# A weight-stationary expert form in two widths (136 and 152 rows) in a hybrid decoder trunk's MoE layer

## What is computed

```
logits = h @ w_router                      # 512 x 8
top_logit, top_e = top_k(logits, 2); gates = softmax(top_logit)
# rows are sorted by expert and padded to blocks of 128
y_block = (silu(x @ w1[e]) * (x @ w3[e])) @ w2[e]     # w1, w3: 1024 x 3584, w2: 3584 x 1024
y = sum over a row's two experts of gate * y_block row
```

## Time and profile before

| | before |
|---|---|
| median of 3 runs | 2075.96 us (2074.44 to 2076.59) |
| the profiled execution | 2074.16 us, of which the span from first to last instruction is 2072.5 us |
| PE busy | 1995.7 us (96%) |
| PE weight loads busy | 1770.0 us (85%) |
| DVE busy | 1576.3 us (76%) |
| ACT busy | 1104.1 us (53%) |
| mean DMA rate | 218 GB/s |

### The profile page before, as it was taken

How to read it: one execution, slowest core, us unless ns; L and a number is a source line. 1 busy time by engine, 2 the same in 40 slices (tenths; PEclk the granted TensorE clock), 3 DMA queues, 4 the chain that set the end, 5 groups by cost and what they waited for, 6 DMA issues and landing times.

```text
span 2072.5 us, 34371 instructions
## 1 busy us (share of the span) xinstructions
PE 1995.7 (96%) x12246; PEld 1770.0 (85%) x12247; DVE 1576.3 (76%) x1964; ACT 1104.1 (53%) x1269; POOL 89.5 (4%) x104
## 2 busy tenths in 40 slices
PE   7999999999999999999999999999999999999993
PEld 6889787877778788999999988888999888999882
DVE  6866535344468677888888899998888998888996
ACT  6532423323345423555555577777555776555773
POOL 0000000000000002100100010101000101000101
PEclk9999999999999999999999999999999999999997
DMA  5312723132312215777777699999777999776983
GB/s 195 105 59 92 265 80 119 64 121 63 119 61 92 71 52 170 250 261 259 250 252 260 231 378 368 364 379 340 270 243 244 340 378 325 254 259 235 375 318 144
DMA packets 218811, 450.97 MB, mean 218 GB/s; under 512 B 13088, under 2 KB 64304, under 8 KB 218768
## 3 DMA queue, kind: packets, MB, share of 16 engines
q1 hardware_dynamic: 210416, 421.05, 58.2%
q0 software_dynamic: 8352, 29.33, 3.8%
HBM read 432.50 MB, written 17.84 MB: 217 GB/s over the span
## 4 chain that ended last, share of the span: by engine, by line
PE 83%; DVE 10%; issue 3%; ACT 2%; DMA 1%; DVEq 0%; POOL 0%; ACTq 0%; SPq 0%; POOLq 0%
PE ps L583 17%; PE ps L585 17%; PE ps L584 17%; PE ps L925 12%; PE ps L942 8%; PE ps L927 5%; PE ps L944 3%; DVE w_lo L1777 2%; DVE w_lo L1774 1%; PE ps L652 1%; ACT w_hi L1189 1%; DVE w_lo L1331 1%; PE ps L607 1%; PE ps L846 1%; DVE ex L1356 0%
## 5 line engine op out<-in xcount | busy, mean ns | idle before, releaser
L1774 DVE TENSOR_TENSOR w_lo<-raw,w_hi 128x1024 fp32r<-128x1024 f32 x340 | 414.5, 1219 | 81.9 <-ACT w_hi L1189 79.5
L925 PE MATMUL ps<-xt,w_hi 128*128 128x320 f32 x1792 | 465.3, 347 | 2.2 <-DVE xt L1788 1.9
L927 PE MATMUL ps<-xt,w_lo 128*128 128x160 f32 x1792 | 424.2, 237 | 0.0
L1189 ACT ACTIVATE w_hi<-raw 128x1024 fp32r<-128x1024 f32 x340 | 357.4, 1051 | 112.6 <-PE ps L927 61.2
L1777 DVE TENSOR_TENSOR w_lo<-raw,w_hi 128x1024 fp32r<-128x1024 f32 x340 | 414.1, 1218 | 0.0
L1191 ACT ACTIVATE w_hi<-raw 128x1024 fp32r<-128x1024 f32 x340 | 356.4, 1048 | 0.0
L927 PEld LDWEIGHTS ps<-xt,w_lo 128*128 128x128 f32 x1792 | 343.1, 191 | 0.1
L925 PEld LDWEIGHTS ps<-xt,w_hi 128*128 128x128 f32 x1792 | 337.2, 188 | 2.8 <-issue 2.7
L583 PE MATMUL ps<-act_hi,w_hi 128*128 128x512 f32 x608 | 242.1, 398 | 5.2 <-DVE act_lo L1375 5.2
L585 PE MATMUL ps<-act_hi,w_lo 128*128 128x512 f32 x608 | 239.9, 395 | 0.0
L584 PE MATMUL ps<-act_lo,w_hi 128*128 128x512 f32 x608 | 239.9, 395 | 0.0
(11 more groups left out here) (330 smaller groups left out, 3174.7 us busy)
## 6 DMA issues: line engine op xcount, KB each, us to landing
raw<-in_moe_w_dram SPq DMA_DIRECT2D x672, 512.0 KB, 5.4
raw<-in_w_in_dram SPq DMA_DIRECT2D x19, 1024.0 KB, 5.1
raw<-in_ffn_w_gate_dram SPq DMA_DIRECT2D x11, 1024.0 KB, 5.3
raw<-in_ffn_w_up_dram SPq DMA_DIRECT2D x11, 1024.0 KB, 5.4
raw<-in_ffn_w_down_dram SPq DMA_DIRECT2D x11, 1024.0 KB, 4.9
raw<-in_w_out_dram SPq DMA_DIRECT2D x8, 1024.0 KB, 5.0
y_rows<-mult POOLq DMA_DIRECT2D x1, 8192.0 KB, 29.5
y_rows<-yacc POOLq DMA_DIRECT2D x8, 512.0 KB, 5.5
```

What stands on the lines that cost most here:

```text
L925: pe.matmul(pairs_of(ps[:, bank, 0:2 * NW]), hi_[:, k % 4, f * P:(f + 1) * P], xt[:, k, :, 0:NW], start=k == 0, stop=False)
L927: last = pe.matmul(ps[:, bank, NW:2 * NW], lo_[:, k % 4, f * P:(f + 1) * P], xt[:, k, 0, 0:NW], start=False, stop=k == KT - 1)
L1189: act.activation(slot_hi[p % 6][:, 0:half], raw6(p)[:, 0:half], ACT.Copy).then_inc(w_hi_half, 1)
L1774: dve.tensor_tensor(slot_lo[p % 6][:, 0:half], raw6(p)[:, 0:half], f32(slot_hi[p % 6][:, 0:half]), ALU.subtract)
```

## The change

The width of the turned form falls from 160 to 152 rows for everything that is allocated, copied, added or multiplied, and its limit on the second block from 32 to 24 rows. On PE alone there are two bodies of the turned item: one streams 152 rows, the other 136. The router's list says which: two more DVE operations in the chain make the flag 2 where the second block has at most 8 rows (`NARROW - P`), and 1 otherwise. The banks keep their layout in steps of `NW`; the narrow body streams the first 136 columns of each of the two halves, so its input and its output of L925 and L942 are two stretches with a gap of 16 columns. In the 152 body the two halves stay adjacent. The columns past 136 that the other engines read in a narrow item hold what was there before, and belong to no row.

```
-NW = P + 32
+NW = P + 24
+NARROW = P + 8
...
-            def turned_up(kind, f, p, c_at):
+            def turned_up(kind, f, p, c_at, nw):
...
-                    pe.matmul(pairs_of(ps[:, bank, 0:2 * NW]), hi_[:, k % 4, f * P:(f + 1) * P],
-                              xt[:, k, :, 0:NW], start=k == 0, stop=False)
-                    last = pe.matmul(ps[:, bank, NW:2 * NW], lo_[:, k % 4, f * P:(f + 1) * P],
-                                     xt[:, k, 0, 0:NW], start=False, stop=k == KT - 1)
+                    pe.matmul(pairs_of(ps[:, bank, 0:2 * NW])[:, :, 0:nw], hi_[:, k % 4, f * P:(f + 1) * P],
+                              xt[:, k, :, 0:nw], start=k == 0, stop=False)
+                    last = pe.matmul(ps[:, bank, NW:NW + nw], lo_[:, k % 4, f * P:(f + 1) * P],
+                                     xt[:, k, 0, 0:nw], start=False, stop=k == KT - 1)
...
-                    pe.matmul(pairs_of(ps[:, bank, 0:2 * NW]), hi_[:, f % 2, d * P:(d + 1) * P],
-                              ht_n[:, f, :, :], start=f == 0, stop=False)
-                    last = pe.matmul(ps[:, bank, NW:2 * NW], lo_[:, f % 2, d * P:(d + 1) * P],
-                                     ht_n[:, f, 0, :], start=False, stop=f == 3)
+                    pe.matmul(pairs_of(ps[:, bank, 0:2 * NW])[:, :, 0:nw], hi_[:, f % 2, d * P:(d + 1) * P],
+                              ht_n[:, f, :, 0:nw], start=f == 0, stop=False)
+                    last = pe.matmul(ps[:, bank, NW:NW + nw], lo_[:, f % 2, d * P:(d + 1) * P],
+                                     ht_n[:, f, 0, 0:nw], start=False, stop=f == 3)
...
             with pe.Fori(0, n_items) as n:
-                with pe.If(pe.snap(turned_next, min_val=0, max_val=1) > 0):
-                    item_turned(n)
+                form = pe.snap(turned_next, min_val=0, max_val=2)
+                with pe.If(form > 0):
+                    with pe.If(form > 1):
+                        item_turned(n, NARROW)
+                    with pe.Else():
+                        item_turned(n, NW)
                 with pe.Else():
                     item_one(n)
...
             link(dve.tensor_tensor(w3v[3], n_row, over_n(last_item), ALU.is_equal))
+            link(dve.scalar_tensor_tensor(rest_of, rest_of, float(NARROW - 2 * P), turned_e, ALU.is_le, ALU.mult))
+            link(dve.tensor_tensor(turned_e, turned_e, rest_of, ALU.add))
             link(dve.tensor_tensor(w3v[3], w3v[3], over_n(turned_e), ALU.mult))
```

More of the change, by code:

```diff
@@ L932, in turned_up, with turned_down @@
                     last.then_inc(w_used, 2)
-            def turned_down(d, p, c_at):
+            def turned_down(d, p, c_at, nw):
                 bank = (4 + d) % 8
@@ L949, in turned_down, with item_turned @@
                     last.then_inc(y_ps, 1)
-            def item_turned(n):
+            def item_turned(n, nw):
                 pe.wait_ge(xt_lo_done, n * 2 + 2)
@@ L956, in item_turned @@
                     for f in range(4):
-                        turned_up(kind, f, 2 * kind, n * IP)
+                        turned_up(kind, f, 2 * kind, n * IP, nw)
                 with pe.Fori(0, EC - 1) as c:
@@ L963, in item_turned @@
                             pe.wait_ge(y_added, q * 4 + (f // 2 + 3))
-                        turned_up(0, f, 4, at_)
+                        turned_up(0, f, 4, at_, nw)
                     for f in range(4):
@@ L967, in item_turned @@
                             pe.wait_ge(us_ready, q * 2 + (f // 2 + 1))
-                        turned_up(1, f, 6, at_)
+                        turned_up(1, f, 6, at_, nw)
                     pe.wait_ge(ht_lo_done, q * 2 + 2)
@@ L972, in item_turned @@
                             pe.wait_ge((us_ready, gs_ready)[d // 4], q * 2 + (3 + d % 4 // 2))
-                        turned_down(d, 8, at_)
+                        turned_down(d, 8, at_, nw)
                 q, at_ = n * EC + (EC - 1), n * IP + 6 * (EC - 1)
@@ L981, in item_turned @@
                         pe.wait_ge(xt_lo_done, n * 2 + (d // 2 + 1))
-                    turned_down(d, 4, at_)
+                    turned_down(d, 4, at_, nw)
                 for half in range(2):
@@ L1309, in _ @@
             with act.Fori(0, n_items) as n:
-                turned_form = act.value_load(items[0:1, bass.ds(n + 48, 1)], min_val=0, max_val=1)
+                turned_form = act.value_load(items[0:1, bass.ds(n + 48, 1)], min_val=0, max_val=2)
                 with act.If(turned_form > 0):
@@ L2009, in _ @@
             with dve.Fori(0, n_items) as n:
-                turned_form = dve.value_load(items[0:1, bass.ds(n + 48, 1)], min_val=0, max_val=1)
+                turned_form = dve.value_load(items[0:1, bass.ds(n + 48, 1)], min_val=0, max_val=2)
                 with dve.If(turned_form > 0):
```

## The result

The changed kernel takes 2101.34 us (median of 6 runs, 2095.24 to 2103.24) against 2075.78 us: a ratio of 1.0119 (95% interval 1.0106 to 1.0133), 25.6 us slower. Forecast was 25.1 us faster. Its profiled execution took 2102.46 us with a span of 2100.6 us, 28.1 us over the span of before. The list holds eight items, as before.

What follows compares the result with a forecast made beforehand. PE's pairs bound steady chunks, the PE-DVE-ACT-DVE-PE loop narrow ones, ACT/DVE the heads. Items 25.7 us, less 0.2 for the first head, less 0.4 added: 25.1 us saved, 2050.9 us median (2049.1 profiled), chance 0.69; range 2042 to 2062.

Steps and rivals of the forecast that it cites:

- The step that failed: PE's code at changes of form between items: the second body was given no cost, against 0.23 us of issue seen before.
- the gap in the moving pattern: Narrow body's 16-column gap: taken as zero; rivals 10 ns a pair in both bodies (0.07) or 49 ns narrow (0.03 with code).
- code stood for part of 0.03: Chance that the kernel gets slower by the gap or by code: 0.03 for the two together.
- No split, eight items: Router's list: no expert is split, eight items before and after; rival of a split at expert 0, 2121 us, chance 0.03.
- Price of a pair: PE's hi and lo matmuls: lo-to-hi step falls with columns, hi-to-lo stays 0.11 us; 236.8 ns narrow, 250.6 wide.
- The rival in which both streams shrink: PE's pairs: the short stream gets cheaper too, 226.5 ns narrow and 247.2 wide, 2043 us; chance 0.06.
- The gap rule: Skill's N/2.4 + 2.5 ns for a stream of N columns: both steps shrink, 30 ns a narrow pair, 10 a wide.
- The loop PE, DVE, ACT, DVE, PE: Steady chunks: permit at P+17.70, P being PE's next gate start; narrow chunk waits 0.65, takes 23.38 us; wide 24.06, no wait.
- Head: Item's first matmul to first passing of PE's wait for DVE, bound by ACT/DVE: saves 1.47 us narrow, 0.70 wide.
- Tail: From PE's end of chunk 5's down to the next item: saves 0.42 us narrow, 0.25 wide.
- Router's chain, +0.4 us: Two added, waited-for DVE operations +0.38 less 0.07 for narrower xt operations, plus PE's branch below 0.1: together +0.4 us.
- The terms together: Items' savings from head, five chunks and tail: 8.6 us narrow, 4.25 wide, twice each, 25.7 together.

Runs made afterwards that it cites:

- one_152: Kernel before with only the turned width cut from 160 to 152 rows, one turned body, no second body on PE: 2059.58 us, ratio 0.9930.
- one_136: Kernel before with one turned body streaming 136 rows in all four turned items, rows 137 to 152 of experts 0 and 6 left out: 2047.27 us, ratio 0.9859.
- act_136: one_136 with ACT making the hi part of piece 10 (6 in the head) before the second Silu instead of behind it: 2020.08 us, ratio 0.9744.
- dead_11f: Kernel before with eleven never-selected groups of matmuls added in PE's item loop, 1589 instructions in all: 2118.93 us, ratio 1.0204.
- dead_128: Kernel before with four never-selected groups of matmuls added in PE's item loop, 1363 instructions in all: 2079.85 us, ratio 1.0025.
- dead_9f: Kernel before with nine never-selected groups of matmuls added in PE's item loop, 1525 instructions in all: 2082.32 us, ratio 1.0031.

## Why the prediction was wrong

**The step that failed** is a single sentence: "A second body on PE is more code; the change of form between items costs 0.23 us of 'issue' though it goes to other code, so I set nothing." The row was right, the inference was not. In the kernel before, a change of form goes to other code that is still there. That row says nothing of a jump to code that isn't, and the page had a line to ask: a queue of PE's code with 29 packets, none of them after 1009.9 us, although seven more items ran. That the loop lived without fetching was a property of its size, and the change took it from 1231 to 2098 instructions across a limit between 1525 and 1589. The price was 43.3 us of branches, with some loss of clock on top. An estimate from the runs agrees: two items as wide as in one_152 (15.0 us gained for four) and two as narrow as in one_136 (27.3 for four) would gain about 21 us together; the changed kernel lost 25.6, so the second body cost some 47. I bounded the gap in the moving pattern from both sides and this step not at all; among the rivals, code stood for part of 0.03.

The Trainium skill ("Runtime: NRT & Kernel Launch", section "Instruction fetch mechanics") says that code comes in blocks of 16 KB, that fetching ahead is sequential, and that a taken branch whose target isn't in the window waits for a fetch. The trace agrees: 0.90 MB in 55 packets is 16 KB each, and the long branches go with them. The Trainium skill gives PE room for 2048 instructions there; here 1589 were already too many to come back over, and the measurement decides. How this limit comes about, no run here shows.

**The rest, point by point.**

- *No split, eight items*: right.
- *Price of a pair*: the short step stays at its floor, the long one goes by columns. Loads of the changed kernel in a narrow item:

```profile
1099.97 0.19 PEld L928 LDWEIGHTS ps<-xt,w_lo 128*128 128x128 f32 x1
1100.10 0.19 PEld L926 LDWEIGHTS ps<-xt,w_hi 128*128 128x128 f32 x1
1100.20 0.19 PEld L928 LDWEIGHTS ps<-xt,w_lo 128*128 128x128 f32 x1
...
1100.92 0.19 PEld L928 LDWEIGHTS ps<-xt,w_lo 128*128 128x128 f32 x1
```

  Four pairs in 0.95 us, 237.5 ns against 236.8 forecast. The gap of 16 columns costs nothing. Wide pairs cost 24.26/96 = 252.7 ns, not 250.6: my line between 320 and 512 columns was 2 ns off at 304, which is 0.2 us a chunk. The rival in which both streams shrink falls, for the short step didn't move. The gap rule that the prediction quoted beside it was read too widely: the Trainium skill ("TensorE: Matmul & The Clock Gate", section "Back-to-back issue gap") gives it for single matmuls, and says that where each matmul has a load, both set the step. The trace agrees with the latter in so far as the short step stays at the load's 0.10 to 0.11 us.
- *The loop PE, DVE, ACT, DVE, PE*: right, and shown by act_136. Narrow chunks 23.46 us (23.38 forecast), PE's wait 0.43 us (0.65).
- *Head*: the gain of 1.5 us was there in the narrow item that kept its clock (31.47 + 9.27 = 40.74 us against 42.24). PE's wait there is 2.34 us in two parts, where 2.5 was forecast. Where the clock fell behind it, the gain was nothing, as in two heads of one_136. That a longer wait can cost more than itself I had not priced.
- *Tail*: one_136 has 20.95 us for the last two downs and the tail in its fifth item, 8.21 of them the down of chunk 5, so 12.74 against 13.17: 0.43 saved, 0.42 forecast.
- *Router's chain, +0.4 us*: too small to be seen beside the rest.
- *The terms together*: one_152 has neither the second body nor the two operations in the list; the same sum gives it 4 x 4.25 = 17.0 us (measured 15.0).

## What to carry to other kernels

Before a body of a loop is duplicated, look at the code queue on the page: if a loop runs without fetching, its size is a resource like a buffer, and on PE here it ended between 1525 and 1589 instructions. Specialise the innermost stretch that gains, not the whole body, and count instructions before and after. And where a chain over other engines stands just behind the bound (0.64 us of slack in a chunk of 24.72), a shorter matmul is worth only what that chain gives; with 136 rows in all four items, one exchange on ACT was worth 27 us, as much as the narrower width had been.

## What the runs showed of the hardware that I had not expected

- Code that is jumped over counts as much as code that runs: dead_11f runs nothing new but the second branch and loses 43 us. 64 instructions fewer, and 6 us remain.
- A jump to code that isn't at hand took between 3.3 and 9.3 us, and a boundary can cross two or three of them: 13.1 us of PE idle before 1942.56 us, from two.
- A first pass can pay too: in dead_128 the first jump over the single body, which takes 0.4 us in the kernel before, took 3.4 us; in dead_9f PE stood 4.8 us once in straight code.
- Two waits of PE of 0.9 to 1.2 and 1.4 us, 3.5 us apart in a head, were followed by 3.4 us at 1.2 GHz in three heads (one in the changed kernel, two in one_136) and by none in two with the same waits (1490.2 us in the changed kernel, 1753.1 us in one_136). Single waits there of 0.7 to 1.2 us never were; the one of 3.3 us, in the first head of one_136, was followed by 6.8. What decides between the three and the two is open.
- Two branches in a chunk of 23 us, targets at hand, cost nothing that shows. PE's sequencer runs ahead of its matmuls: in the kernel before, the way back of the chunk loop is taken at 1074.9 us, and the first matmul behind it starts at 1077.08.
- Still open: why the stalls differ between 3.3 and 9.3 us, and why 1633 instructions with a choice inside the item lose more than 2098. In the changed kernel's four long branches of 3.3 to 3.8 us a packet starts about 1 us after the branch, in the four of 6.1 to 9.3 us the first one starts 2.2 to 5.3 us after it. That the limit is a whole number of packets was not tested; 1536 would be six. Nor was the loop moved against the packets' boundaries at one length, so the two bounds hold for these programs.
